# A mixture of 16,384 experts: routing starts inside the last projections, and 192 of 256 tokens are scattered by indirect transfers

## The chip, the core and the metric

The kernel runs on one core of a Trainium2 chip. The core's engines work side by side, each through its own queue of instructions: TensorE (PE) multiplies matrices, VectorE (DVE) and ScalarE (ACT) work elementwise, GpSimd (POOL) issues the indirect DMAs and does some elementwise work, SyncE (SP) issues the other DMAs. They wait for one another through semaphores. The metric is the device time of one execution in microseconds (us); less is better.

## What is computed

One decoder layer on 256 tokens of width 1024, all in float32: a mixer (a gated linear recurrence beside block-sparse attention), cross-attention into 256 memory tokens, and a channel mixer of 128 x 128 single-neuron experts (PEER). The change touches the last alone, of which this is the core:

```python
def peer_ffn(xn, w_q, sub_keys, u, v):            # T = 256 tokens, 8 heads, 128 keys, top 16
    q = (t @ w_q).reshape(T, PEER_HEADS, 2, PEER_HALF)
    s = jnp.einsum('thpd,hpnd->thpn', q, sub_keys)
    s_top, i_top = lax.top_k(s, PEER_TOPK)
    cand_s = s_top[:, :, 0, :, None] + s_top[:, :, 1, None, :]          # 16 x 16 sums
    cand_i = i_top[:, :, 0, :, None] * PEER_KEYS + i_top[:, :, 1, None, :]
    best_s, pos = lax.top_k(cand_s, PEER_TOPK)
    ids = jnp.take_along_axis(cand_i, pos, axis=-1)
    gates = jax.nn.softmax(best_s, axis=-1)
    act = jax.nn.gelu(jnp.einsum('td,ted->te', x_c, u[ids_c]), approximate=False)
    return jnp.einsum('te,ted->td', g_c * act, v[ids_c])
```

A token thus needs 8 heads x 16 ranks = 128 of the 16,384 experts, each with a gate.

## The kernel before

**Dense experts.** The kernel computes all experts for all tokens. A matrix A of 16,384 experts x 256 tokens (act_w, 128 keys of 128 experts) gets gelu(u t), is multiplied by a map of gates that is zero where a token doesn't use an expert, and is then multiplied with v. Every float32 product is made of three matmuls: both operands are split into a high part, which ACT copies in a rounded type, and a low part, which DVE subtracts.

**Projections.** 38 units of 256 columns (L1109), 48 matmuls each. SP loads a unit's weights into one of four buffers, ACT writes the high part (wsp, L395), DVE the low one (L714; GpSimd for two units). Units 30 to 37 make the PEER queries. Then come 32 matmuls of key scores (L1258), which ACT copies out, and the residual as a seed in the accumulators of V.

**Stage U, 128 keys.** Each key takes 24 matmuls of 256 columns (L1273 to L1275). SP loads two keys' weights at a time (raw), ACT writes the high part (hl, L625) and the GELU (L630), DVE the low part (hl, L937). Four buffers hold split keys.

**Routing, woven into U.** DVE does the top-16 work in 64 parts, four per head and tile of 128 tokens: the 16 best rows, the 16 best columns (L941 to L953), the 256 candidate sums and their best (L957 and on), and index and logit (L962 to L978). A table puts 8 parts into 11 keys. ACT takes the exponential, DVE normalizes it (gate_norm, L984 to L986).

- Tile 0: one indirect DMA on GpSimd (L370) adds 128 tokens' gates of one head and rank into a map in HBM (wmap, 8 MB, zeroed by four stores of SP). That is 128 DMAs, and before each head GpSimd waits for the head before (s_scattered), since two heads may meet in one cell.
- Tile 1: after key 92 PE transposes the gates (L1310); from key 95 on, each key carries one of 32 groups of four tokens: DVE and ACT write one-hot rows and columns (oh_i L994, oh_j L642 and L646, each fourth on DVE), PE multiplies them (L1299), DVE applies the result to A (place, L1008). Columns of keys that come later get their GELU through a buffer (late, L634 and L1016).

**Stage V.** For every two keys SP loads a block of the map (wblk, L306 and L314) as soon as all scatters have landed, GpSimd weighs A with it (L376), ACT and DVE write A's high and low parts (whl, L677 and L1050), and PE does 12 matmuls of 512 columns per key (L1324). Then follow the final norm and the store.

The order on each engine is the order in which its block of code issues. The functions that the diff touches:

Of the kernel before, what the change touches and what calls it, by code (L numbers as in the profile page):

```python
# [58 lines left out]
NGRP = P // GRP  # L59
NZERO = 4  # L60
WBK = 2
NWB = KEYS // WBK
BATCHES = ((0, 1), (1, 3), (3, PH))
# [4 lines left out]
def build(nc, x, mem, par, wa, wx, w, keys_t, u_t, v, g_final, wmap, out):  # L68
    ctx = ExitStack()
    with ctx:  # L70
# [30 lines left out]
        zeros = at("zeros", m + 2 * K, [512])  # L101
        krow = at("krow", m, [3, P])
# [3 lines left out]
        kt3 = at("kt3", m, [3, P])  # L106
        late = at("late", m + 1536, [2, P])
        wblk = at("wblk", m + 2560, [2, WBK, P])
# [9 lines left out]
        sumf = at("sumf", m + 2 * K + 1280, [TOPK])  # L118
        m += 4 * K + 512
        gate = at("gate", m, [PH, TOPK]); m += 512  # L120
        widx = at("widx", m, [PH, TOPK], U32); m += 512
# [59 lines left out]
        s_sca = sem("s_scattered")  # L181
        s_kt, s_kte = sem("s_key_cols_mm"), sem("s_key_cols")
        s_ojd = sem("s_onehot_j_dve")
# [42 lines left out]
        def part_key(n):  # L226

            return -(-11 * (n + 1) // 8) - 1

        def pass_key(n):  # L230

            return part_key(4 * n + 3)
# [6 lines left out]
        wm = wmap.rearrange("(i j t) o -> i j (t o)", i=KEYS, t=P)  # L239
# [9 lines left out]
        def dve_j(g):  # L249

            return (g + 1) // 4

        def placed(j):

            return GRP * max(0, min(NGRP, j + 1 - ROUTE0))

# [4 lines left out]
        def _(sp):  # L261
# [17 lines left out]
            sp.wait_ge(s_const, 9)  # L279
# [4 lines left out]
            for u in range(WRAW, NU):  # L284
                unit(u)
                if u % 2 == 0 and u // 2 - U_CK // 2 in range(NZERO):
                    z = (u - U_CK) // 2
                    n = KEYS * P // 512 // NZERO
                    sp.dma_start(wz[:, z * n:z * n + n], zeros[:].unsqueeze(1).broadcast_to([P, n, 512])).then_inc(s_zero, 16)
                if u == U_PQ + 4:  # L290
                    sp.dma_start(keys[:], keys_t).then_inc(s_keys, 16)
# [12 lines left out]
            sp.wait_ge(s_sca, 16 * TOPK * PH)  # L304
# [18 lines left out]
        def _(pool):  # L323
# [15 lines left out]
            nc.gpsimd.iota(tcol[:, 0:1], pattern=[[1, 1]], base=0, channel_multiplier=1,  # L339
                           allow_small_or_imprecise_dtypes=True).then_inc(s_const, 1)  # L340
# [23 lines left out]
            for b, (h0, h1) in enumerate(BATCHES):  # L364
                pool.wait_ge(s_gr, b + 1)
                for h in range(h0, h1):
                    if h:
                        pool.wait_ge(s_sca, 16 * TOPK * h)
                    for k in range(TOPK):
                        nc.gpsimd.indirect_dma_start(  # L370
                            out=wmap, out_offset=bass.IndirectOffsetOnAxis(ap=widx[:, h, k:k + 1], axis=0),
                            in_=gate[:, h, k:k + 1], in_offset=None, compute_op=ALU.add).then_inc(s_sca, 16)
# [17 lines left out]
        def _(act):  # L390
# [77 lines left out]
            act.wait_ge(s_const, 9)  # L468
# [142 lines left out]
            for u in range(U_PQ, NU):  # L611
                unit(u)
            sr = srow[:].rearrange("p (t h) a k -> p t (h a k)", t=TT)
            for n in range(8):
                act.wait_ge(s_ks, n + 1)
                nc.scalar.activation(sr[:, n // 4, 512 * (n % 4):512 * (n % 4) + 512], bank[n % 4][:], ACT.Copy).then_inc(s_ke, 1)


# [18 lines left out]
            def onehots_j(g):  # L637
                t0, slot = group_token(g), g % 2
# [6 lines left out]
                act.wait_ge(s_ojq, g + 1 - dve_j(g))  # L645
                nc.scalar.activation(oh_j[:, slot], oh_j[:, slot], ACT.Relu, scale=-1.0, bias=ones[:, 0:1]).then_inc(s_oja, 1)  # L646

            act.wait_ge(s_pv, HEADS + CHEADS)
            for k in range(4):
                split_high(k, 16 if k % 2 == 0 else None, (s_seed, 1) if k == 2 else None, s_uh)  # L650
            act.wait_ge(s_zero, 16 * NZERO)

            exps = 0
            for j in range(KEYS):
# [6 lines left out]
                if exps < len(BATCHES) and j == pass_key(BATCHES[exps][1] - 1) + 2:  # L661
                    h0, h1 = BATCHES[exps]
                    act.wait_ge(s_rt, h1)
                    nc.scalar.activation(gate[:, h0:h1], gate[:, h0:h1], ACT.Exp).then_inc(s_ge, 1)
                    exps += 1
                if j == pass_key(TT * PH - 1) + 1:
                    act.wait_ge(s_rt, TT * PH)
                    nc.scalar.activation(krow[:, 2], krow[:, 2], ACT.Exp).then_inc(s_ge, 1)
                if j == WEAVE:
                    act.wait_ge(s_kt, 1)  # L670
                    nc.scalar.activation(kt3[:].rearrange("p a t -> p (a t)"), bank[2][:, 0:3 * P], ACT.Copy).then_inc(s_kte, 1)
                    act.wait_ge(s_kte, 1)
                if 0 <= j - (ROUTE0 - 2) < NGRP and (j - (ROUTE0 - 2)) % 4 < 3:
                    onehots_j(j - (ROUTE0 - 2))

            def a_high(j, slot):
                nc.scalar.activation(whl[:, slot, 0], act_w[:, ds(j, 1)].rearrange("p o t -> p (o t)"), ACT.Copy).then_inc(s_Wh, 1)  # L677

            split_high(3, None, (s_um, KEYS), s_vh, second=True)
            act.wait_ge(s_gw, NGRP)  # L680
            for k in range(4):
                if k % WBK == 0:
                    act.wait_ge(s_A, k // WBK + 1)
                a_high(k, k)
# [17 lines left out]
        def _(dve):  # L702
# [228 lines left out]
            for u in range(U_PQ, NU):  # L931
                unit(u)


# [12 lines left out]
            def route_part(n, part):  # L947

                t, h = n // PH, n % PH
                if part < 2:  # L950
                    best16(srow[:, PH * t + h, part], rwork[:], part)
                    if t == 0:
                        link(V.tensor_scalar(topf[:, part], topi[:, part], float(P * (1 if part else KEYS)), None, ALU.mult))  # L953
                    else:
                        link(V.tensor_copy(topf[:, part], topi[:, part]))
# [5 lines left out]
                else:  # L961
# [7 lines left out]
                    if t == 0:  # L969
                        link(V.tensor_reduce(sumf[:], eq[:].rearrange("p a k b -> p k a b"), XY, ALU.add))  # L970
                        link(V.tensor_scalar(widx[:, h], sumf[:], tcol[:, 0:1], None, ALU.add))
                        logits = gate[:, h]
                    else:
                        ks = slice(TOPK * h, TOPK * h + TOPK)
                        link(V.tensor_reduce(krow[:, 0:2, ks], eq[:], X, ALU.add))
                        logits = krow[:, 2, ks]
                    V.tensor_scalar(logits, topv[:, 2], topv[:, 2, 0:1], None, ALU.subtract).then_inc(s_rt, 1)

            def gate_norm(n, ex):

                dve.wait_ge(s_ge, n + 1)
                k = ex.shape[1]
                gs = stat[:, GS:GS + k]
                link(V.tensor_reduce(gs, ex, X, ALU.add))  # L984
                link(V.reciprocal(gs, gs))
                V.tensor_tensor(ex, ex, gs.unsqueeze(2).broadcast_to([P, k, TOPK]), ALU.mult).then_inc(s_gr, 1)  # L986

            def onehots_i(g):
                t0, slot = group_token(g), g % 2
# [7 lines left out]
                if g % 4 == 3:  # L997
                    V.tensor_tensor(oh_j[:, slot], iota[:].unsqueeze(1).broadcast_to([P, GRP, P]),
                                    kt3[:, 1, t0:t0 + GRP].unsqueeze(2).broadcast_to([P, GRP, P]), ALU.is_equal).then_inc(s_ojd, 1)

            def place(g):

                dve.wait_ge(s_gm, g + 1)
                j0, c = ROUTE0 + g, P + group_token(g)
# [13 lines left out]
            for k in range(4):  # L1018
                split_low(k, s_ul, (s_uh, k + 1))
            dve.wait_ge(s_ke, 8)  # L1020
            dve.wait_ge(s_zero, 16 * NZERO)


            parts = normed = 0
            for j in range(KEYS):
                if j < KEYS - 4:
                    split_low(j % 4, s_ul, (s_uh, j + 5))
                elif j < KEYS - 1:
                    split_low(j % 4, s_vl, (s_vh, j + 5 - KEYS), second=True)
                if normed < len(BATCHES) and j == pass_key(BATCHES[normed][1] - 1) + 4:  # L1030
                    h0, h1 = BATCHES[normed]
                    gate_norm(normed, gate[:, h0:h1])
                    normed += 1
                if j == pass_key(TT * PH - 1) + 3:
                    gate_norm(normed, krow[:, 2].rearrange("p (h k) -> p h k", k=TOPK))
# [3 lines left out]
                if 0 <= j - ROUTE0 < NGRP:  # L1039
                    place(j - ROUTE0)  # L1040
# [4 lines left out]
                if 0 <= j - (ROUTE0 - 2) < NGRP:  # L1045
                    onehots_i(j - (ROUTE0 - 2))
# [5 lines left out]

            split_low(3, s_vl, (s_vh, 4), second=True)
            for k in range(4):
                a_low(k, k)
# [318 lines left out]
```

## Time and profile before

| | |
|---|---|
| median of three runs | 1067.56 us (1065.86 to 1069.15) |
| the profiled execution's own time | 1069.02 us |
| its span in the trace | 1067.0 us |
| mean granted TensorE clock | 0.987 |
| busy: PE / DVE / ACT / POOL | 97 / 68 / 54 / 27% |
| projections up to the key scores | 0 to 293 us |
| stage U | 304 to 707 us |
| stage V and the end | 710 to 1067 us |

A row of a timeline gives start and duration in us, engine, line, operation and tiles, and in brackets the idle time of that engine ahead of it and what ended it. A count (x8) behind a row joins like instructions.

### The profile page before, as it was taken

How to read it: one execution, taken by the hardware profiler on the slowest of the kernel's cores; microseconds unless marked ns; L12 is line 12 of the kernel's file. 1: busy time of each engine (PE TensorE's matmuls, PEld its weight loads, DVE VectorE, ACT ScalarE, POOL GpSimd, SP SyncE). 2: the span in 40 equal slices, each digit the busy share in tenths (PEclk: the TensorE clock that was granted, in tenths of full speed). 3: DMA queues.
4: the chain of work that ended last, by engine and by line, in shares of the span. 5: the costliest groups of instructions: out<-in, count | busy, mean ns of one | idle time of the engine just before them, and what ended most of it. 6: DMA issues, size and time to landing. Idle time of an engine off the chain costs nothing.

```text
span 1067.0 us, 19322 instructions
## 1 busy us (share of the span) xinstructions
PE 1036.6 (97%) x7019; PEld 960.4 (90%) x7019; DVE 729.4 (68%) x1439; ACT 574.8 (54%) x988; POOL 289.0 (27%) x215
## 2 busy tenths in 40 slices
PE   6999999999999999999999999989999999999997
PEld 6988899899999999999999999978888888888886
DVE  5765566544349999999997888865555555555554
ACT  6784555544365544534446778745445554455543
POOL 1000001010002788577778650011111111111110
PEclk9998999998999999999999999989999999999999
DMA  9598444426234766666666553446666566666662
GB/s 318 166 316 287 148 142 148 145 80 194 83 119 158 197 160 196 178 176 185 181 186 182 137 157 129 149 158 214 213 213 216 211 219 217 221 221 221 217 214 95
DMA packets 92480, 196.56 MB, mean 184 GB/s; under 512 B 23569, under 2 KB 70673, under 8 KB 75921
## 3 DMA queue, kind: packets, MB, share of 16 engines
q1 hardware_dynamic: 74000, 195.87, 52.9%
q0 software_dynamic: 18432, 0.07, 3.9%
q8 instruction: 28, 0.46, 0.2%
q14 instruction: 20, 0.16, 0.0%
HBM read 186.42 MB, written 9.50 MB: 184 GB/s over the span
## 4 chain that ended last, share of the span: by engine, by line
PE 70%; DVE 20%; DMA 4%; ACT 4%; issue 1%; SPq 0%; DVEq 0%; ACTq 0%
PE acc L1324 33%; PE acc L1109 19%; DVE hl L937 6%; PE bank L1273 4%; PE bank L1274 4%; PE bank L1275 4%; DMA raw<-u_t 4%; PE bank L1299 3%; DVE hl3u L937 2%; DVE topv L943 1%; DVE eq L965 1%; DVE eq L968 1%; ACT hl L625 1%; DVE topi L944 1%; DVE topi L945 1%
## 5 line engine op out<-in xcount | busy, mean ns | idle before, releaser
L937 DVE TENSOR_TENSOR hl<-raw,hl 128x1024 fp32r<-128x1024 f32 x192 | 234.4, 1226 | 152.6 <-ACT hl L625 150.8
L625 ACT ACTIVATE hl<-raw 128x1024 fp32r<-128x1024 f32 x192 | 203.3, 1059 | 232.6 <-PE acc L1324 130.3
L1324 PE MATMUL acc<-hl,whl 128*128 128x512 f32 x1152 | 269.2, 392 | 3.2 <-DVE whl L1050 3.2
L370 POOL DMA_INDIRECT wmap<-gate,widx x128 | 219.7, 1716 | 173.7 <-DVE gate L986 109.8
L1324 PEld LDWEIGHTS acc<-hl,whl 128*128 128x128 f32 x1152 | 218.0, 189 | 48.9 <-DVE hl3v L937 3.3
L1273 PE MATMUL bank<-xt,hl 128*128 128x256 f32 x768 | 220.8, 287 | 0.6 <-DVE hl L937 0.5
L1274 PE MATMUL bank<-xt,hl 128*128 128x256 f32 x768 | 217.8, 284 | 0.0
L1275 PE MATMUL bank<-xt,hl 128*128 128x256 f32 x768 | 217.8, 284 | 0.0
L376 POOL TENSOR_TENSOR act_w<-act_w,wblk 128x256 f32 (+1 forms) x64 | 51.4, 803 | 364.2 <-DMA wblk<-wmap 296.9
L1273 PEld LDWEIGHTS bank<-xt,hl 128*128 128x128 f32 x768 | 147.9, 193 | 1.5 <-issue 1.2
L1274 PEld LDWEIGHTS bank<-xt,hl 128*128 128x128 f32 x768 | 148.0, 193 | 0.2 <-issue 0.2
L1275 PEld LDWEIGHTS bank<-xt,hl 128*128 128x128 f32 x768 | 147.8, 192 | 0.0
L714 DVE TENSOR_TENSOR wsp<-wraw,wsp 128x2048 fp32r<-128x2048 f32 x35 | 80.2, 2290 | 77.1 <-ACT wsp L395 76.9
L1109 PE MATMUL acc<-xt,wsp 128*128 128x256 f32 x960 | 120.7, 289 | 2.5 <-DVE xt L735 2.5
L1109 PEld LDWEIGHTS acc<-xt,wsp 128*128 128x128 f32 x960 | 119.4, 197 | 3.6 <-issue 3.5
L395 ACT ACTIVATE wsp<-wraw 128x2048 fp32r<-128x2048 f32 x35 | 66.9, 1913 | 85.1 <-PE acc L1109 85.1
L1324 PE MATMUL acc<-hl3v,whl 128*128 128x512 f32 x384 | 92.4, 389 | 0.0
L1324 PEld LDWEIGHTS acc<-hl3v,whl 128*128 128x128 f32 x384 | 72.1, 188 | 15.0
L630 ACT ACTIVATE act_w<-bank 128x256 f32<-128x256 f32 (+11 forms) x128 | 46.4, 363 | 66.4 <-PE bank L1275 66.1
L1273 PE MATMUL bank<-xt,hl3u 128*128 128x256 f32 x256 | 73.2, 286 | 0.2 <-DVE hl3u L937 0.2
L1275 PE MATMUL bank<-xt,hl3u 128*128 128x256 f32 x256 | 72.4, 283 | 0.0
L1274 PE MATMUL bank<-xt,hl3u 128*128 128x256 f32 x256 | 72.4, 283 | 0.0
(219 smaller groups left out, 1325.4 us busy)
## 6 DMA issues: line engine op xcount, KB each, us to landing
raw<-u_t SPq DMA_DIRECT2D x64, 1024.0 KB, 4.9
raw<-v SPq DMA_DIRECT2D x64, 1024.0 KB, 4.9
wraw<-w_in SPq DMA_DIRECT2D x9, 1024.0 KB, 8.3
wmap<-zeros SPq DMA_DIRECT2D x4, 2048.0 KB, 11.6
wraw<-w_pq SPq DMA_DIRECT2D x8, 1024.0 KB, 5.3
wblk<-wmap SPq DMA_DIRECT2D x64, 128.0 KB, 4.6
wraw<-w_ck SPq DMA_DIRECT2D x4, 1024.0 KB, 7.7
wraw<-w_cv SPq DMA_DIRECT2D x4, 1024.0 KB, 6.5
```

What stands on the lines that cost most here:

```text
L370: nc.gpsimd.indirect_dma_start(out=wmap, out_offset=bass.IndirectOffsetOnAxis(ap=widx[:, h, k:k + 1], axis=0), in_=gate[:, h, k:k + 1], in ...
L376: nc.gpsimd.tensor_tensor(aw, aw, wblk[:, q], ALU.mult).then_inc(s_A, 1)
L395: nc.scalar.activation(wsp[:, u % 2, 0], wraw[:, u % WRAW], ACT.Copy).then_inc(s_wh, 1)
L625: nc.scalar.activation(eslot(k, 0, second), raw[:, k // 2, k % 2], ACT.Copy).then_inc(ready, 1)
L630: last = nc.scalar.activation(aw[:, 0:T - n], ubank(j)[:, 0:T - n], ACT.Gelu)
L714: V.tensor_tensor(wsp[:, u % 2, 1], wraw[:, u % WRAW], wsp[:, u % 2, 0].bitcast(F32), ALU.subtract).then_inc(s_wl, 1)
L937: V.tensor_tensor(eslot(k, 1, second), raw[:, k // 2, k % 2], eslot(k, 0, second).bitcast(F32), ALU.subtract).then_inc(ready, 1)
L1109: last = pe.matmul(dst, a, b, start=(c == c0 and n == 0), stop=(c == c1 - 1 and n == 2))
L1273: pe.matmul(dst, uh[:, c], xt[:, c, 0], start=(c == 0), stop=False)
L1274: pe.matmul(dst, uh[:, c], xt[:, c, 1], start=False, stop=False)
L1275: last = pe.matmul(dst, ul[:, c], xt[:, c, 0], start=False, stop=(c == DC - 1))
L1324: last = pe.matmul(acc[:, 2 * t + n], a, b[:, 512 * n:512 * n + 512], start=False, stop=last_key and k == 2, skip_group_check=True)
```

## The change

- **Key scores and routing start earlier.** The scores of a head (now both tiles at once) are made right behind the projection unit that follows it, so the keys are loaded in the projections already. 14 of the 64 route parts (3.5 heads of tile 0) and two gate steps stand on DVE between the weight splits of units 30 to 37 and the first operand splits of U. The other parts keep their pace of 8 in 11 keys and so end at key 68 instead of 87.
- **192 tokens are scattered.** The map is 192 tokens wide (WT; 12 MB, zeroed by six stores). Tile 0 goes as two sets of 64 tokens x 2 ranks, so a DMA still carries 128 cells and a head takes two times 8; tokens 128 to 191 go as two sets of 32 tokens x 4 ranks, two times 4 for a head. That makes 192 DMAs. Each set has a semaphore, and a head waits for the same set of the head before. The gate step (gates) also computes the address and copies gates and addresses into the sets' layout: 8 small copies for tile 0, 16 for tile 1.
- **One-hots for the last 64 tokens alone**, 16 groups, one at every second key from 95 to 125; all their columns on ACT.
- **Stage V's blocks and the weighing** are 192 tokens wide instead of 128, and SP waits for all four sets.
- **The high and low parts of A for the first four keys** are written behind key 126, ahead of the last key's GELU and split, once their weighing and the last one-hot group are done.

```diff
-NZERO = 4
+HT = P // 2
+NGRP = HT // GRP
+WT = P + HT
+NZERO = 6
-BATCHES = ((0, 1), (1, 3), (3, PH))
+SETS = ((0, 0, 64, 8), (0, 64, 64, 8), (1, 0, 32, 4), (1, 32, 32, 4))
+BATCHES = ((0, 0, 1), (0, 1, 3), (0, 3, 5), (0, 5, PH), (1, 0, PH))
+PARTS0 = 14
...
-            return -(-11 * (n + 1) // 8) - 1
+            return -(-11 * (n - PARTS0 + 1) // 8) - 1
...
-            sp.wait_ge(s_sca, 16 * TOPK * PH)
+            for k, (_, _, _, nr) in enumerate(SETS):
+                sp.wait_ge(s_sca[k], 16 * nr * PH)
...
-            for b, (h0, h1) in enumerate(BATCHES):
+            for b, (t, h0, h1) in enumerate(BATCHES):
                 pool.wait_ge(s_gr, b + 1)
                 for h in range(h0, h1):
-                    if h:
-                        pool.wait_ge(s_sca, 16 * TOPK * h)
-                    for k in range(TOPK):
...
+                    for k in (2 * t, 2 * t + 1):
+                        nr = SETS[k][3]
+                        if h:
+                            pool.wait_ge(s_sca[k], 16 * nr * h)
+                        for r in range(nr):
...
-                aw = act_w[:, ds(b * WBK, WBK), 0:P]
+                aw = act_w[:, ds(b * WBK, WBK), 0:WT]
...
+            def gates(b):
+
+                t, h0, h1 = BATCHES[b]
+                n, ks = h1 - h0, slice(TOPK * h0, TOPK * h1)
+                link(V.scalar_tensor_tensor(dest[:, ks], krow[:, t, 0, ks], float(KEYS), krow[:, t, 1, ks], ALU.mult, ALU.add))
+                link(V.tensor_scalar(dest[:, ks], dest[:, ks], float(WT), tcol[:, t:t + 1], ALU.mult, ALU.add))
+                dve.wait_ge(s_ge, b + 1)
...
+                link(V.tensor_tensor(ex, ex, gs.unsqueeze(2).broadcast_to([P, n, TOPK]), ALU.mult))
+                for k in (2 * t, 2 * t + 1):
+                    _, t0, nt, nr = SETS[k]
+                    for r in range(TOPK // nr):
...
+                        V.tensor_copy(set_ranks(gate, k)[p, h0:h1], ex[src, :, rs])
+                        last = V.tensor_copy(set_ranks(widx, k)[p, h0:h1], to[src, :, rs])
+                last.then_inc(s_gr, 1)
...
+            for u in range(U_PQ, NU - 2):
+                unit(u)
+                if u == U_PQ + 4:
+                    gates(0)
+                    route_parts(6, 7)
+                elif u > U_PQ:
+                    p0 = 2 * (u - U_PQ - 1) if u < U_PQ + 5 else 7
+                    route_parts(p0, p0 + 2)
+            split_low(0, s_ul, (s_uh, 1))
+            route_parts(9, 12)
+            split_low(1, s_ul, (s_uh, 2))
+            route_parts(12, PARTS0)
+            gates(1)
+            for k in (2, 3):
...
+                if j == KEYS - 2:
+                    act.wait_ge(s_gw, NGRP)
+                    for k in range(4):
+                        if k % WBK == 0:
+                            act.wait_ge(s_A, k // WBK + 1)
+                        a_high(k, k)
...
+            for u in range(U_PQ + 1, NU):
+                unit(u, xt)
+                if u < NU - 1:
+                    key_scores(u - U_PQ - 1)
```

Three places show what stands in a row on an engine. First GpSimd, where the scatter begins; s_gates counts gate steps, s_scattered the landed DMAs (with a number: those of a set). Before:

```order
L370 DMA wmap<-gate,widx 2097152x1 [waits s_gates,s_zeroed]
L370 DMA wmap<-gate,widx 2097152x1 x15
L370 DMA wmap<-gate,widx 2097152x1 [waits s_scattered,s_gates]
L370 DMA wmap<-gate,widx 2097152x1 x15
L370 DMA wmap<-gate,widx 2097152x1 [waits s_scattered]
```

And now:

```order
L380 DMA wmap<-gate,widx 3145728x1 [waits s_gates,s_zeroed]
L380 DMA wmap<-gate,widx 3145728x1 x15
L380 DMA wmap<-gate,widx 3145728x1 [waits s_scattered0,s_gates]
L380 DMA wmap<-gate,widx 3145728x1 x7
L380 DMA wmap<-gate,widx 3145728x1 [waits s_scattered1]
L380 DMA wmap<-gate,widx 3145728x1 x7
```

The wait for the head before now looks back over eight DMAs of the other set.

Second VectorE, in the last projection units. Before, weight splits (wsp) run straight into the operand splits of U (hl), and the first top-16 (topv) comes behind six of them:

```order
L714 TENSOR_TENSOR wsp<-wraw,wsp 128x2048 [waits s_w_high] x7
L937 TENSOR_TENSOR hl<-raw,hl 128x1024 [waits s_u_high] x2
L937 TENSOR_TENSOR hl_54<-raw,hl_54 128x1024 [waits s_u_high]
L937 TENSOR_TENSOR hl3u<-raw,hl3u 128x1024 [waits s_u_high]
L937 TENSOR_TENSOR hl<-raw,hl 128x1024 [waits s_u_high,s_zeroed,s_key_rows]
L937 TENSOR_TENSOR hl<-raw,hl 128x1024 [waits s_u_high]
L941 MAX topv<-srow 128x8
```

Now, between two weight splits, this is the first gate step, which follows six route parts (two of its four pairs of copies are shown):

```order
L735 TENSOR_TENSOR wsp<-wraw,wsp 128x2048 [waits s_w_high,s_dve_chain]
L993 SCALAR_TENSOR_TENSOR dest<-krow 128x16
L994 TENSOR_SCALAR dest<-dest,tcol 128x16 [waits s_dve_chain]
L999 TENSOR_REDUCE stat<-krow 128x1 [waits s_gate_exp,s_dve_chain]
L1000 RECIPROCAL stat<-stat 128x1 [waits s_dve_chain]
L1001 TENSOR_TENSOR krow<-krow,stat 128x16 [waits s_dve_chain]
L1006 COPY gate<-krow 64x8 [waits s_dve_chain]
L1007 CAST widx<-dest 64x8
L1006 COPY gate<-krow 64x8
L1007 CAST widx<-dest 64x8
```

The first weight split of a later unit now waits behind such steps, and so do U's operand splits.

Third ScalarE, at the end of U. Before:

```order
L625 ACTIVATE hl_54<-raw 128x1024 [waits s_u_mm,s_raw1]
L630 ACTIVATE act_w<-bank 128x128 [waits s_u_mm]
L634 ACTIVATE late<-bank 128x128 [waits s_late_gelu_used]
L625 ACTIVATE hl3v<-raw 128x1024 [waits s_u_mm]
L677 ACTIVATE whl<-act_w 128x256 [waits s_weighed,s_route_placed]
L677 ACTIVATE whl<-act_w 128x256
L677 ACTIVATE whl<-act_w 128x256 [waits s_weighed]
L677 ACTIVATE whl<-act_w 128x256
```

And now:

```order
L639 ACTIVATE hl_54<-raw 128x1024 [waits s_u_mm,s_raw1]
L679 ACTIVATE whl<-act_w 128x256 [waits s_weighed,s_route_placed]
L679 ACTIVATE whl<-act_w 128x256
L679 ACTIVATE whl<-act_w 128x256 [waits s_weighed]
L679 ACTIVATE whl<-act_w 128x256
L644 ACTIVATE act_w<-bank 128x192 [waits s_u_mm]
L648 ACTIVATE late<-bank 128x64 [waits s_late_gelu_used]
L639 ACTIVATE hl3v<-raw 128x1024 [waits s_u_mm]
```

The four copies of A (whl), with their waits for the weighing and for the last one-hot group, now stand ahead of the last GELU and the last high part.

## Rows read from the trace of the kernel before

**Rows 1.** The page: DMA engines' busy tenths in 40 slices; longest chain by line.

```profile
DMA  9598444426234766666666553446666566666662
...
PE acc L1324 33%; PE acc L1109 19%; DVE hl L937 6%; PE bank L1273 4%; PE bank L1274 4%; PE bank L1275 4%; DMA raw<-u_t 4%; PE bank L1299 3%; DVE hl3u L937 2%; DVE topv L943 1%; DVE eq L965 1%; DVE eq L968 1%; ACT hl L625 1%; DVE topi L944 1%; DVE topi L945 1%
```

**Rows 2.** Timeline of ScalarE at the start of U (start us, us, engine, line).

```profile
312.92 0.39 ACT L630 ACTIVATE act_w<-bank 128x256 f32<-128x256 f32 x1 [0.86 <-PE bank L1275]
...
315.80 0.38 ACT L630 ACTIVATE act_w<-bank 128x256 f32<-128x256 f32 x1 [1.55 <-PE bank L1275]
```

**Rows 3.** Timeline of TensorE at the joints and at two one-hot groups.

```profile
293.44 7.38 PE L1258 MATMUL bank<-keys,qpt 128*128 128x128 f32 x64 [0.84 <-ACT qpt L408]
...
575.83 0.85 PE L1310 MATMUL bank<-ident,krow 128*128 128x128 f32 x3 [1.92 <-DVE krow L986]
...
695.61 1.06 PE L1299 MATMUL bank<-oh_j,oh_i 128*128 128x128 f32 x8
...
699.38 1.06 PE L1299 MATMUL bank<-oh_j,oh_i 128*128 128x128 f32 x8
...
710.23 6.07 PE L1324 MATMUL acc<-hl,whl 128*128 128x512 f32 x14 [3.17 <-DVE whl L1050]
```

**Rows 4.** Windows: us, busy PE PEld DVE ACT POOL (instructions), PEclk, DMA, GB/s.

```profile
575.80:579.50 3.70, 3.67 (x18) 3.67 (x19) 1.11 (x1) 0.75 (x1) 3.09 (x3) 0.54 1.05 352
...
716.00:1060.00 344.00, 344.00 (x1520) 284.82 (x1518) 195.40 (x252) 172.14 (x253) 49.88 (x62) 1.00 0.59 208
```

**Rows 5.** Timeline of GpSimd: the first transfer, two around 580, the last.

```profile
338.53 1.69 POOL L370 DMA_INDIRECT wmap<-gate,widx  x1 [99.12 <-DVE gate L986]
...
580.47 2.01 POOL L370 DMA_INDIRECT wmap<-gate,widx  x1 [0.30 <-issue]
582.79 2.09 POOL L370 DMA_INDIRECT wmap<-gate,widx  x1 [0.30 <-issue]
...
631.19 1.54 POOL L370 DMA_INDIRECT wmap<-gate,widx  x1 [0.30 <-issue]
```

**Rows 6.** Timeline of VectorE: last weight split, first routing and gate step.

```profile
283.13 2.29 DVE L714 TENSOR_TENSOR wsp<-wraw,wsp 128x2048 fp32r<-128x2048 f32 x1 [3.47 <-ACT wsp L395]
...
313.25 0.29 DVE L941 MAX8 topv<-srow 128x8 f32<-128x128 f32 x1
...
315.15 1.23 DVE L937 TENSOR_TENSOR hl<-raw,hl 128x1024 fp32r<-128x1024 f32 x1
...
321.18 0.42 DVE L957 TENSOR_TENSOR cand<-topv 128x256 f32<-128x256 f32 x1
...
324.01 1.22 DVE L937 TENSOR_TENSOR hl<-raw,hl 128x1024 fp32r<-128x1024 f32 x1
...
325.15 0.17 DVE L962 TENSOR_SCALAR posu<-topi 128x16 uint32<-128x16 uint32 x1
...
328.24 1.22 DVE L937 TENSOR_TENSOR hl<-raw,hl 128x1024 fp32r<-128x1024 f32 x1
...
337.44 0.18 DVE L986 TENSOR_TENSOR gate<-gate,stat 128x16 f32<-128x16 f32 x1
```

**Rows 7.** Waits of GpSimd at the transfers: us in all, times, longest.

```profile
POOL wmap L370 <- issue: 43.4, 120, 3.6
...
POOL wmap L370 <- DMA wmap<-gate,widx: 20.4, 6, 4.2
```

**Rows 8.** Groups by line on GpSimd: busy us, mean ns, idle before.

```profile
L370 POOL DMA_INDIRECT wmap<-gate,widx x128 | 219.7, 1716 | 173.7 <-DVE gate L986 109.8 <-issue 43.4 <-DMA wmap<-gate,widx 20.4
...
L376 POOL TENSOR_TENSOR act_w<-act_w,wblk 128x256 f32 (+1 forms) x64 | 51.4, 803 | 364.2 <-DMA wblk<-wmap 296.9 <-ACT late L634 67.3
```

**Rows 9.** Timeline of VectorE beside the two transfers of rows 5.

```profile
579.85 1.23 DVE L937 TENSOR_TENSOR hl<-raw,hl 128x1024 fp32r<-128x1024 f32 x1 [2.94 <-ACT hl L625]
...
582.24 1.23 DVE L937 TENSOR_TENSOR hl<-raw,hl 128x1024 fp32r<-128x1024 f32 x1 [1.17 <-ACT hl L625]
```

**Rows 10.** DMAs of line L314 (the blocks of the map): issue to landing.

```profile
DMA to landing us min/median/max: 4.3/4.6/8.6
```

More of the change, by code:

```diff
@@ L105, in build @@
         m += 8 * K
-        kt3 = at("kt3", m, [3, P])
-        late = at("late", m + 1536, [2, P])
-        wblk = at("wblk", m + 2560, [2, WBK, P])
+        kt3 = at("kt3", m, [3, HT])
+        late = at("late", m + 768, [2, HT])
+        wblk = at("wblk", m + 1280, [2, WBK, WT])
         cand = at("cand", m, [256])
@@ L117, in build @@
         topf = at("topf", m + 2 * K + 1152, [2, TOPK])
-        sumf = at("sumf", m + 2 * K + 1280, [TOPK])
+        dest = at("dest", m + 3 * K + 512, [PH * TOPK])
         m += 4 * K + 512
-        gate = at("gate", m, [PH, TOPK]); m += 512
-        widx = at("widx", m, [PH, TOPK], U32); m += 512
+        gate = at("gate", m, [WT]); m += 768
+        widx = at("widx", m, [WT], U32); m += 768
         tcol = at("tcol", m, [8]); m += 32
@@ L180, in build @@
         s_zero = sem("s_zeroed")
-        s_sca = sem("s_scattered")
+        s_sca = [sem(f"s_scattered{i}") for i in range(len(SETS))]
         s_kt, s_kte = sem("s_key_cols_mm"), sem("s_key_cols")
-        s_ojd = sem("s_onehot_j_dve")
         s_oi, s_ojq, s_oja, s_gm, s_gw, s_fx = (sem(n) for n in (
@@ L610, in _, with key_rows, gate_exp @@
             after_norm(U_PQ - 1, 3, "ln_ffn")
[L611 to L616, printed above, removed]
+            sr = srow[:].rearrange("p (t h) a k -> p t h (a k)", t=TT)
+            def key_rows(h):
+                act.wait_ge(s_ks, h + 1)
+                nc.scalar.activation(sr[:, :, h], bank[h % 4][:].rearrange("p (t n) -> p t n", t=TT), ACT.Copy).then_inc(s_ke, 1)
+            def gate_exp(b):
+                t, h0, h1 = BATCHES[b]
+                act.wait_ge(s_rt, PH * t + h1)
+                ex = krow[:, t, 2, TOPK * h0:TOPK * h1]
+                nc.scalar.activation(ex, ex, ACT.Exp).then_inc(s_ge, 1)
             def split_high(k, landed, free, ready, second=False):
@@ L930, in _ @@
             unit(U_PQ - 1)
-            for u in range(U_PQ, NU):
-                unit(u)
             def split_low(k, ready, have, second=False):
@@ L950, in route_part @@
                 if part < 2:
+                    if part == 0 and t == 0:
+                        dve.wait_ge(s_ke, h + 1)
                     best16(srow[:, PH * t + h, part], rwork[:], part)
[L952 to L955, printed above, removed]
+                    link(V.tensor_copy(topf[:, part], topi[:, part]))
                 elif part == 2:
@@ L1029, in _ @@
                     split_low(j % 4, s_vl, (s_vh, j + 5 - KEYS), second=True)
[L1030 to L1035, printed above, removed]
+                if batches < len(BATCHES) and j == batch_key(batches) + 4:
+                    gates(batches)
+                    batches += 1
                 if parts < 4 * TT * PH and j == part_key(parts):
@@ L1245, in _, with key_scores, seed @@
             unit(U_PQ, xt, (s_tl, 3 * DC))
-            for u in range(U_PQ + 1, NU):
-                unit(u, xt)
             pe.wait_ge(s_keys, 16)
-            wevac(pe, NU - 1)
-            for t in range(TT):
-                for b in range(4):
-                    n = 4 * t + b
-                    if n >= 4:
-                        pe.wait_ge(s_ke, n - 3)
-                    for k in range(4):
-                        hp = 4 * b + k
-                        last = pe.matmul(bank[b][:, P * k:P * k + P], qpt[:, hp, P * t:P * t + P], keys[:, hp], start=True, stop=True)
-                    last.then_inc(s_ks, 1)
-            for t in range(TT):
+            def key_scores(h):
+                wevac(pe, U_PQ + h)
+                if h >= 4:
+                    pe.wait_ge(s_ke, h - 3)
+                for t in range(TT):
+                    for a in range(2):
+                        c = T * t + KEYS * a
+                        last = pe.matmul(bank[h % 4][:, c:c + KEYS], qpt[:, 2 * h + a, P * t:P * t + P], keys[:, 2 * h + a],
+                                         start=True, stop=True)
+                last.then_inc(s_ks, 1)
+            def seed(t):
                 for n in range(2):
```

165 lines of the change are left out of this document (81 added, 84 removed).

## The prediction

> **What bounds the kernel now.** I read the page's chain by line first, then TensorE's timeline at the joints between stages, then the queue that the change loads most, GpSimd's. The chain is TensorE nearly throughout: the value stage (acc L1324) 33%, the projections (L1109) 19%, and where VectorE's split (hl L937) stands in the chain, TensorE is busy beside it [rows 1]. So TensorE has a floor of instructions and a few joints where it waits. One U key takes 2.88 us: two GELUs lie that far apart [rows 2]. A key that carries a one-hot group takes 3.77 [rows 3], so a group costs 0.89. Two joints are dear. After key 92 TensorE waits 1.92 us for the last gates, and the granted clock then stands at 0.54 for 3.7 us, near the lower level of 1.2 GHz: 18 matmuls take 3.67 us where 18 x 0.12 = 2.2 is the pace: 1.5 lost, 3.4 together [rows 3, 4]. From U to V it waits 3.17 us, and the first 14 value matmuls take 6.07, where 344 us for 1520 is the pace, 3.2 for 14: 2.9 lost, 6.0 together [rows 3, 4]. GpSimd ends its 128 indirect transfers at 631.19 + 1.54 = 632.7, some 75 us before V asks for them [rows 5]: today it is far off the path.
>
> **What the change takes off TensorE.** 16 of 32 one-hot groups: 16 x 0.89 = 14.2. The wait behind key 92: the last gates now come at DVE's key 72, 20 keys before the transposes, so the 3.4 goes. The 0.84 wait ahead of the key scores [rows 3]: the scores go into the projection units, their 7.38 us and the seeds' time stay, 0.8 goes. The joint U to V: high and low parts of A for keys 0 to 3 move ahead of GELU 127, so 3.2 of wait goes if the weighed activations are there, and the 2.9 of slow clock with it. Together 14.2 + 3.4 + 0.8 + 6.0 = 24.4 us.
>
> **What it puts on VectorE.** In the last units VectorE idles 3.47 of every 5.76 us (3.47 + 2.29) [rows 6]. That is the cover for 14 route parts and two gate steps, and it isn't enough. A top-16 part is 315.15 - 313.25 = 1.90, the candidates' 324.01 - 321.18 = 2.83, the last part 3.09, without its widx step 2.8 [rows 6]. From 283.13 - 4 x 5.76 = 260.1 on, five weight splits (2.29 each, 11.5), 14 parts (8 x 1.90 + 3 x 2.83 + 3 x 2.8 = 32.1), two gate steps and three operand splits (3.5) stand in one row. A gate step is not in the trace as it will be: the old one is three operations of about 0.2 [rows 6]; the new one has 13 small ones, so 0.5 to 3; I take 1.8, 13 at 0.14. The third split is then done at 260.1 + 11.5 + 32.1 + 3.6 + 3.5 + 0.6 of small waits = 311.4. Key 2, whose GELU is at 312.92 in before, starts a key's 2.88 and a little sooner, at 309.8 [rows 2]; now 0.8 earlier, 309.0: a stall of 2.4, with a clock loss like the one above, 1.5. Later gate steps fall into VectorE's fullest stretch, but the parts end at key 68, not 87; this cancels, within 2. So TensorE alone would begin V at 710.2 - 14.2 - 3.4 - 3.2 - 0.8 + 3.9 = 692.5.
>
> **What it puts on GpSimd** decides, I think. 192 transfers stand in for 128. The first follows gate step 0: 260.1 + four weight splits 9.2 + six parts 13.2 + 0.6 + 1.8 = 284.9, and 0.9 on, as 338.53 stands behind the end of the old step at 337.62 [rows 5, 6]: 285.8. From there the queue never runs dry, and the waits for the head before, 20.4 us in six [rows 7], go, since eight (four) transfers of the other set lie between. The mean transfer is 1.72 [rows 8] plus 0.30 of issue, but the shortest are 1.54, 1.84 with the issue [rows 5], and the rest is a mechanism: a transfer that starts while a two-input split runs on VectorE waits for its end. The split at 579.85 ends at 581.08; the transfer of 580.47 ends 1.40 after that, and the next starts at 582.79, 1.71 after it [rows 5, 9]. Three stretches follow.
> (a) To 518 VectorE is full of parts (50 parts 119, 69 splits 84, two steps 3.6, from 312). I take 2.04, the 2.02 of before and a little for the gates: 232 / 2.04 = 114 transfers.
> (b) To 579 (key 93) VectorE has one split a key. A split ends, the next begins 2.88 - 1.23 = 1.65 later, the transfer asks at 1.71, just inside it, and is held to its end again: one transfer a key. Until VectorE has caught up I take 2.3 over 26 us, then 2.88 over 35: 23 transfers.
> (c) To 691, a group every second key: 2.88 + 3.77 = 6.65 hold three transfers (held, free, held), 2.22 each: 50.
> That is 187; five more with VectorE idle at 1.84 end at 700. Longer gaps come on top: issue gaps sum to 43.4 in 120, 7.4 over 0.30 each, the longest 3.6 [rows 7]; 192 transfers make it 11, and what falls into a hold is free: I take 6, bounds 0 and 14. The last ends at 706. Behind it: 3.4 to its landing (20.4 / 6), 4.6 for wblk [rows 10], a weighing of 0.80 x 1.5 = 1.2 [rows 8], and the high and low parts, 0.9 (the old joint's 3.17 less a copy and a split): 10.1. V begins at 716, not 710.2: **5.8 us later**. TensorE has then been idle for 25 us, so the slow first matmuls stay.
>
> The Trainium skill's page "SBUF — State Buffer", in "SBUF: two separate sides", says that VectorE and GpSimd share one port pair as an exclusive lock for a whole instruction, and warns of VectorE's copies in a 2-port mode that keep GpSimd from writing a DMA's descriptors. The trace agrees on the lock, with 1.40 us of a transfer left after the split's end. The warning names the copies alone; by those alone each transfer would take 1.84, the last end at 639, and V begin at 692.5. The rows show two-input splits that hold the queue, so the rows decide.
>
> **What I cost at nothing.** Two more zero stores lie beside the w_out loads, where the DMA engines are 40% busy (slices 5 to 8) [rows 1]; one late weight load there would cost some us. The 50% larger wblk and weighing lie under V, where TensorE is busy 344 of 344 us [rows 4]; a wblk buffer has two key pairs, 10.9 us, for 4.6 + 1.2 and the issue. Exp steps move with their gates, five against four.
>
> **The rivals.** First, on the other side, GpSimd in time: if the holds of (b) and (c) don't lock and 2.02 lasts, 285.8 + 192 x 2.02 + 6 = 680, V is ready at 690 and TensorE's 692.5 counts: 17.7 earlier and no slow clock, 2.9: 1067.6 - 20.6 = 1047. For it: the mean held at 2.02 over a varied trace. Against it: that stretch has routing on VectorE throughout. It decides once the last transfer ends before 682. Second, GpSimd late but by less: no long gaps and 2.0 in (c): end at 690 to 699, V at 700 to 709, time 1057 to 1066. Third, worse: long gaps twice as many, or 2.88 from 518 on: end at 715, V at 725, 1082. Fourth, the early one-hot values don't do what they say: the ACT wait for the weighed pairs now stands ahead of GELU 127 and the last split; behind a late GpSimd all of these queue. That is in the forecast, since V needs the pairs first anyway.
>
> **How the numbers follow.** The profiled execution took 1069.02 with a span of 1067.0, 1.5 above the median, 1067.56. The sum moves the span to 1072.8, the execution to 1074.8, the median to 1073.4; I say 1073. Chances: forecast 0.56, GpSimd in time 0.13, late by less 0.22, worse 0.09. The range reaches to the second and third: 1056 to 1082, leaving out the first and a tail. 0.3%, 3.2 us, is about what a measurement of this kernel can tell from no change. Faster by more than that: 0.13 and half of "late by less", 0.25; within: the rest of it and the forecast's lower part, 0.23; slower: 0.52.
>
> **What the profile after would show.** The first transfer near 286; 114 done by 518; starts 2.88 apart between 545 and 579 and three per 6.65 from there; the last end near 706; then wblk, weighing, and the first value matmul at 716 behind an idle of 25 us. A stall at U key 2 of about 2.4; none behind key 92; 16 groups of 0.89. I am wrong if transfers keep a pace of 2.0 after 518, or if TensorE waits for VectorE for more than 5 us in U.

## The result, and the profile after

The changed kernel takes 1058.97 us (1056.94 to 1061.39) against 1067.68 for the kernel before in the same runs, a ratio of 0.9927 with a 95% interval of 0.991 to 0.9944. It is 0.7% faster where I forecast 0.5% slower. The profiled execution has a span of 1059.6 us against 1067.0.

The chain of the changed kernel, from the page, shows first what happened: GpSimd's transfers (L380) now hold a third of the span, where TensorE and VectorE held it before [rows 1].

```profile
PE 53%; POOL 33%; issue 6%; DVE 4%; ACT 2%; DMA 1%; SPq 0%; DVEq 0%; ACTq 0%; POOLq 0%
PE acc L1362 33%; POOL wmap L380 33%; PE acc L1142 16%; DVE wsp L735 1%; ACT wsp L405 1%; DMA wraw<-w_in 1%; DVE xs L751 1%; PE bank L1246 1%; PE bank L1224 0%; PE bank L1171 0%; DMA wmap<-gate,widx 0%; PE bank L1154 0%; PE bank L1153 0%; PE bank L1112 0%; DMA wblk<-wmap 0%
```

GpSimd's groups and waits of the changed kernel answer [rows 7, 8]. The queue waits for nothing but its own issue between the first transfer and the last; the waits for the head before are gone.

```profile
L380 POOL DMA_INDIRECT wmap<-gate,widx x192 | 350.5, 1825 | 105.9 <-issue 59.9 <-DVE widx L1007 46.1
```

```profile
POOL wmap L380 <- issue: 59.9, 191, 2.0
```

Its timeline, at the start, in the middle of U and at the end, answers [rows 5], and VectorE's beside the middle answers [rows 9]. The first transfer starts at 285.69. In the middle a transfer starts 0.06 behind a split's start, takes 2.58 instead of 1.54, and the next comes 2.88 later, again 0.06 behind a split's start. The last one ends at 696.05.

```profile
285.69 1.69 POOL L380 DMA_INDIRECT wmap<-gate,widx  x1 [46.05 <-DVE widx L1007]
...
563.70 2.58 POOL L380 DMA_INDIRECT wmap<-gate,widx  x1 [0.30 <-issue]
566.58 2.58 POOL L380 DMA_INDIRECT wmap<-gate,widx  x1 [0.30 <-issue]
569.46 2.58 POOL L380 DMA_INDIRECT wmap<-gate,widx  x1 [0.30 <-issue]
...
694.43 1.62 POOL L380 DMA_INDIRECT wmap<-gate,widx  x1 [0.30 <-issue]
700.18 1.94 POOL L386 TENSOR_TENSOR act_w<-act_w,wblk 128x384 f32<-128x384 f32 x2 [4.13 <-DMA wblk<-wmap]
```

```profile
563.64 1.22 DVE L954 TENSOR_TENSOR hl<-raw,hl 128x1024 fp32r<-128x1024 f32 x1 [1.66 <-ACT hl L639]
566.52 1.23 DVE L954 TENSOR_TENSOR hl3u<-raw,hl3u 128x1024 fp32r<-128x1024 f32 x1 [1.66 <-ACT hl3u L639]
```

TensorE's timeline at U's key 2, at key 33 and at the joint to V answers [rows 3]. It waits 3.63 and 1.90 for VectorE's splits and 7.72 for the first value operands, which wait for the map.

```profile
312.33 0.38 PE L1314 MATMUL bank<-xt,hl 128*128 128x256 f32 x1 [3.63 <-DVE hl L954]
...
405.38 0.38 PE L1314 MATMUL bank<-xt,hl 128*128 128x256 f32 x1 [1.90 <-DVE hl L954]
...
702.55 9.74 PE L1362 MATMUL acc<-hl,whl 128*128 128x512 f32 x29 [7.72 <-DVE whl L1061]
```

So the start of V moved from 710.23 to 702.55, 7.7 us, nearly the whole change of the span (7.4). It is made of 1.3 from an earlier first key (less than executions of one kernel differ by), 10.9 from a shorter U (403.4 to 392.4), and 4.6 given back in the wait before V (3.17 to 7.72).

### The profile page after: what moved, and what is told of

Read it like the earlier page. It is cut to its first block, busy times and chain, and to the rows that moved or that the text cites. A ratio compares the mean times of both kernels' runs of the same rounds, so it can differ in the third digit from the quotient of the medians.

```text
span 1059.6 us, 19013 instructions
## 1 busy us (share of the span) xinstructions
PE 1020.5 (96%) x6891; PEld 944.7 (89%) x6891; DVE 703.6 (66%) x1388; ACT 559.7 (53%) x948; POOL 434.1 (41%) x280
## 4 chain that ended last, share of the span: by engine, by line
PE 53%; POOL 33%; issue 6%; DVE 4%; ACT 2%; DMA 1%; SPq 0%; DVEq 0%; ACTq 0%; POOLq 0%
PE acc L1362 33%; POOL wmap L380 33%; PE acc L1142 16%; DVE wsp L735 1%; ACT wsp L405 1%; DMA wraw<-w_in 1%; DVE xs L751 1%; PE bank L1246 1%; PE bank L1224 0%; PE bank L1171 0%; DMA wmap<-gate,widx 0%; PE bank L1154 0%; PE bank L1153 0%; PE bank L1112 0%; DMA wblk<-wmap 0%
## 5 line engine op out<-in xcount | busy, mean ns | idle before, releaser
L380 POOL DMA_INDIRECT wmap<-gate,widx x192 | 350.5, 1825 | 105.9 <-issue 59.9
L386 POOL TENSOR_TENSOR act_w<-act_w,wblk 128x384 f32 (+1 forms) x64 | 65.6, 1026 | 279.5 <-DMA wblk<-wmap 279.5
```

Of the source, the lines that this page charges most:

```text
L380: nc.gpsimd.indirect_dma_start(out=wmap, out_offset=bass.IndirectOffsetOnAxis(ap=set_ranks(widx, k)[:, h, r:r + 1], axis=0), in_=set_ranks ...
```

## Experiments

My theory was that the last indirect transfer sets the start of V, and that VectorE's two-input splits set the pace of the transfers. The rivals were that TensorE's own time, or something else at the end of U, sets it, and that the pace of one transfer a key has another cause. The projections end up to 3 us earlier or later from one execution to the next, so the traces are compared from U's first matmul on. The last column runs from the start of the first value matmul to the start of the fifteenth. All numbers are us:

| kernel | time | U's first to V's first matmul | last transfer's end, from U's first | wait before V | first 14 value matmuls |
|---|---|---|---|---|---|
| before | 1066.6 to 1067.7 | 406.5 | 329.0 | 3.17 | 5.9 |
| changed | 1058.97 | 400.2 | 393.7 | 7.72 | 6.1 |
| changed, 16 transfers fewer | 1051.8 | 392.4 | 358.1 | 0.43 | 3.3 |
| changed, early A operands undone | 1058.67 | 398.0 | 390.7 | 4.76 | 5.7 |
| changed, halved splits | 1050.06 | 393.3 | 365.0 | 0.50 | 3.3 |
| changed, second gate step later | 1056.59 | 398.8 | 392.5 | 7.55 | 5.3 |
| halved, 12 early parts | 1046.3 | 388.9 | 362.5 | 0.5 | 3.3 |
| halved, 12 early parts, slower pace | 1042.31 | 384.2 | 365.2 | 0.50 | 3.3 |
| the same, early A operands undone | 1046.39 | 386.9 | 365.2 | 3.17 | 6.0 |
| before, early A operands alone | 1062.37 | 404.3 | 329.2 | 0.65 | 3.3 |

### Sixteen transfers fewer

```diff
-                for h in range(h0, h1):
+                for h in range(h0, h1 - 2 * t):
```

(SyncE's count of landed transfers is lowered to match.)

> The changed kernel without the last 16 of its 192 indirect transfers (heads 6 and 7 of tokens 128 to 191 get no gate, so that part of the output is left out). Theory: the value stage begins when the last transfer has landed. Then the queue ends near 661 instead of 696, TensorE goes from U to V without a wait worth naming (under 1 us, at 695 instead of 702.55), the slow first value matmuls go as well, and the time is 1048 to 1052. Rival: the 7.7 us wait has another cause (the block load, the weighing, the order on ScalarE); then V stays at 702.5 and the time at 1059.

The time is 1051.8 us, a ratio of 0.9857 (0.9833 to 0.9882) to the kernel before. The last transfer ends at 659.09. TensorE's timeline at the joint:

```profile
693.36 8.43 PE L1362 MATMUL acc<-hl,whl 128*128 128x512 f32 x36 [0.43 <-DVE whl L1061]
```

The wait is 0.43 and the slow first matmuls are gone: the granted clock is 1.00 from 693.4 to 697.0. Nothing else at the end of U was changed, so the wait of 7.72 was for the transfers and what follows the last of them; the rival falls.

### Early operands of A undone

```diff
             split_high(3, None, (s_um, KEYS), s_vh, second=True)
+            act.wait_ge(s_gw, NGRP)
+            for k in range(4):
+                if k % WBK == 0:
+                    act.wait_ge(s_A, k // WBK + 1)
+                a_high(k, k)
```

(The same loop at key 126 goes, and VectorE's with it.)

> The changed kernel with the high and low parts of A for keys 0 to 3 put back behind the last key's GELU and split. Theory (the indirect transfers set the start of V): nothing is gained or lost, V at 702.5 within 0.5, time within 2 us of 1059. Rival (the early split is worth the 3 to 6 us that I gave to this joint): V some 2 to 3 us later, time 1062 to 1065.

1058.67 us against 1058.97 is no difference: this part of the change does nothing while the map is late. V's own start is at 698.90, outside the half microsecond that I allowed: U began 1.5 earlier and the last transfer ended 2.9 earlier as counted from there, in this one execution. V follows it by 7.3 us, against 6.5 with the early operands, so they save 0.8 behind the last transfer, which the times don't show.

### Halved splits

```diff
+                n = D // pieces
+                for i in range(pieces - 1):
+                    c = slice(n * i, n * i + n)
+                    V.tensor_tensor(eslot(k, 1, second)[:, c], raw[:, k // 2, k % 2, c], eslot(k, 0, second)[:, c].bitcast(F32),
+                                    ALU.subtract)
...
-                    split_low(j % 4, s_ul, (s_uh, j + 5))
+                    split_low(j % 4, s_ul, (s_uh, j + 5), pieces=PIECES if j >= 70 else 1)
```

> The changed kernel with VectorE's operand split of the keys from 74 on issued as two instructions of 512 columns instead of one of 1024. Theory (a transfer that starts while a two-input VectorE instruction runs is held to its end, which locks the queue to one transfer per 2.88 us key): the hold is at most 0.6, starts in the stretch 555 to 584 lie about 1.9 apart instead of 2.88, the last transfer ends near 680 and V begins at 695; time 1048 to 1052. Rival (one transfer per key comes from something else of a key's period, such as the 1 MB weight loads): starts stay 2.88 apart, V stays at 702 and the time at 1059.

1050.06 us, a ratio of 0.9847 (0.9828 to 0.9867). The last transfer ends 28.7 us earlier from U's first matmul on, V waits 0.50, with all 192 transfers there. The end, 665.8, is earlier than the 680 that I expected, since beside the groups the pace fell as well, from 2.2 to 1.9. GpSimd's and VectorE's timelines between 556 and 563 show the mechanism:

```profile
556.78 1.97 POOL L381 DMA_INDIRECT wmap<-gate,widx  x1 [0.31 <-issue]
559.06 1.54 POOL L381 DMA_INDIRECT wmap<-gate,widx  x1 [0.30 <-issue]
560.91 1.54 POOL L381 DMA_INDIRECT wmap<-gate,widx  x1 [0.30 <-issue]
562.75 1.77 POOL L381 DMA_INDIRECT wmap<-gate,widx  x1 [0.30 <-issue]
```

```profile
556.65 0.69 DVE L958 TENSOR_TENSOR hl<-raw,hl 128x512 fp32r<-128x512 f32 x1 [1.59 <-ACT hl L640]
557.26 0.68 DVE L961 TENSOR_TENSOR hl<-raw,hl 128x512 fp32r<-128x512 f32 x1
...
562.41 0.69 DVE L958 TENSOR_TENSOR hl<-raw,hl 128x512 fp32r<-128x512 f32 x1 [1.59 <-ACT hl L640]
```

The transfer of 556.78 starts inside the first half, which ends at 557.34, and ends 1.41 after it, at 558.75, although the second half runs until 557.94: it slips in at the end of one instruction, and is not held by the next. Three transfers now go with two keys: 15 start between 555 and 584, 1.94 apart, where the changed kernel has 11, 2.88 apart. The weight loads and the key's 2.88 us are as before, so the rival falls. The halves cost VectorE 0.15 us a key (2 x 0.69 against 1.23), where it is idle anyway.

Halving shortens the instruction and leaves its two inputs, so by itself it doesn't show that the inputs matter. The rows of the changed kernel bear on that. All 70 transfers that start at least 0.05 us after a split's start and 0.14 before its end end 1.40 to 1.43 after that split. In the routing there are two instructions of the same length, a compare with two inputs (L981) and a reduction with one (L986). Three transfers start inside the compare, with 0.44 to 0.61 of it left, and take 1.86 to 2.02; five start inside the reduction, with 0.40 to 0.57 left, and all take 1.54. One of each, VectorE's row first:

```profile
470.17 0.69 DVE L981 TENSOR_TENSOR eq<-posf,iota 128x512 f32<-128x512 f32 x1
470.25 2.02 POOL L380 DMA_INDIRECT wmap<-gate,widx  x1 [0.30 <-issue]
...
486.90 0.69 DVE L986 TENSOR_REDUCE krow<-eq 128x32 f32<-128x512 f32 x1
487.05 1.54 POOL L380 DMA_INDIRECT wmap<-gate,widx  x1 [0.30 <-issue]
```

### The second gate step later

```diff
-            split_low(1, s_ul, (s_uh, 2))
-            route_parts(12, PARTS0)
-            gates(1)
-            for k in (2, 3):
+            for k in (1, 2, 3):
                 split_low(k, s_ul, (s_uh, k + 1))
+            route_parts(12, PARTS0)
...
+                if j == 0:
+                    gates(1)
```

> The changed kernel with the first four operand splits of U ahead of route parts 12 and 13, and the second gate step behind key 0's split. Theory: the stall of 3.6 us at U's key 2 shrinks below 1.5 and U ends 3 to 5 us earlier, but the indirect transfers end where they did (696 within 2), so V begins at 702 within 2 and the time stays 1059 within 2. Rival (TensorE's own time sets the start of V): the time falls with U's end, to 1054 to 1056.

The stall at key 2 goes, but others take its place, at keys 7, 17, 18 and 55, and U is 1.2 us shorter, not 3 to 5. Part of this expectation failed: the stalls that came elsewhere, in the stretch that VectorE's routing fills up to key 68, took back most of the gain. The groups of TensorE's waits for splits in this run sum to 5.3, where the changed kernel has the 5.5 of its two:

```profile
PE acc L1362 <- DVE whl L1059: 7.5, 1, 7.5
PE bank L1314 <- DVE hl L954: 4.5, 4, 1.8
...
PE bank L1314 <- DVE hl3u L954: 0.8, 2, 0.4
```

By the clock of the trace V is at 698.19 and the last transfer's end at 691.87, outside the 2 us around 702 and 696 that I allowed; U began 3.0 earlier, and from there the transfers end within 1.2 of the changed kernel. V still waits 7.55 for the map and begins 6.3 behind the last transfer, so it is still GpSimd that sets its start. 1056.59 us lies beside the rival's 1054 to 1056, 2.4 under the changed kernel, but the intervals of the two (0.9888 to 0.9942, and 0.991 to 0.9944) overlap, so no gain is shown; it is the trace that speaks against the rival, not the time.

### Twelve early parts, and a slower pace

With the splits halved the last transfer ends 28 us ahead of V. The path behind it takes 6 to 7, so some 21 us are to spare, and these two give VectorE's work more room.

```diff
-PARTS0 = 14
+PARTS0 = 12
```

> The kernel with the halved operand splits (from key 74 on), and with 12 instead of 14 route parts ahead of U, at the same pace of 8 in 11 keys. With GpSimd in time, TensorE's own time counts, and there the stall at U's key 2 (3.8, and 1.6 of slow clock behind it) is the largest loss. Theory: VectorE has two parts (3.8 us) less ahead of key 2, so that stall goes; but 8 parts and 11 splits (32.7 us) don't fit into 11 keys (31.7), so some of it comes back later as short stalls, as in the run with the late gate step. U takes 390 to 391 us instead of 392.8, time 1047 to 1050. Rival: the stalls do not come back; U 387.5, time 1045.

1046.3 us, and U 4.4 us shorter than with the halves alone, between the theory and its rival: stalls come back at keys 21, 26, 36 and 37, 3.2 us together (the one of 1.12 is put down to ScalarE's GELU, the others to VectorE's splits), less than what goes at keys 2, 33 and 77, 6.0 of waits and 1.6 of slow clock (the expectations name the last two by the key ahead, 32 and 76). Then:

```diff
-            return -(-11 * (n - PARTS0 + 1) // 8) - 1
+            return -(-12 * (n - PARTS0 + 1) // 8) - 1
```

> As the run with 12 parts, and the route parts at 8 in 12 keys (halved splits from key 82 on). Theory: 8 parts and 12 splits (33.9 us) fit into 12 keys (34.6), so the stalls at keys 2, 32 and 76 go; U takes 384 to 386 us; tile 1's gates come near 540, when tile 0's transfers are just done, and the last transfer ends near 670, still in time; V at 685 to 687; time 1041 to 1045. Rival: the later gates let GpSimd run dry or end too late, V behind a wait again, time 1050 or more.

1042.31 us, a ratio of 0.9775 (0.975 to 0.98), and 1040.76 on another chip:

> The kernel with halved splits, 12 early parts and 8 parts in 12 keys once more, beside the run with the early operand split undone on the same chip: 1042 within 1.5 us.

(ratio 0.9758, 0.9734 to 0.9782). This is the version that beats both the kernel before and the changed one. TensorE's waits show that none is left for a split in U, and 0.5 before V; the chain, from the page, is TensorE's nearly alone.

```profile
PE acc L1369 <- DVE whl L1068: 0.5, 1, 0.5
```

```profile
PE 93%; DVE 3%; ACT 2%; DMA 1%; issue 0%; SPq 0%; DVEq 0%; ACTq 0%
```

### Early operands of A, where the map is in time

First this part of the change alone, in the kernel before:

```diff
+                if j == KEYS - 2:
+                    act.wait_ge(s_gw, NGRP)
+                    for k in range(4):
+                        if k % WBK == 0:
+                            act.wait_ge(s_A, k // WBK + 1)
+                        a_high(k, k)
```

(VectorE's four splits move in the same way.)

> The kernel before, with one part of the change alone: high and low parts of A for keys 0 to 3 written behind key 126, ahead of the last GELU and split. By my term of 6.0 us for this joint (3.2 of wait, 2.9 of slow clock) the time would be 1061. By the rows of before the last one-hot group is applied at 706.7, so ScalarE's four copies and VectorE's four splits end near 708.5, with V's first matmul at 707.6 to 708.3 instead of 710.23; whether a wait of 1 us still brings the slow clock is open: 1062 if not, 1065 if so.

1062.37 us, ratio 0.9962 (0.9947 to 0.9977): 4.2 us. From U's first matmul on V comes 2.2 earlier, and the first value matmuls run at full clock. Then undone in the best version:

> The kernel with halved splits, 12 early parts and 8 parts in 12 keys, with the early operand split undone: the same edit that changed nothing while GpSimd was late. Theory: with the map in time, the order on ScalarE and VectorE at the end of U counts, as in the kernel before: TensorE waits about 3 us between U and V (0.50 with the early split) and the first 14 value matmuls take about 6 us instead of 3.3; time 1046 to 1048 against 1042.3. Rival: the joint has other slack by now; time within 1.5 us of 1042.3.

1046.39 us against 1040.76 on the same chip: 5.6 us. TensorE's timelines at the joint, the kernel before with it:

```profile
705.27 8.41 PE L1326 MATMUL acc<-hl,whl 128*128 128x512 f32 x36 [0.65 <-DVE whl L1027]
```

and the best version without it:

```profile
689.32 11.16 PE L1367 MATMUL acc<-hl,whl 128*128 128x512 f32 x36 [3.17 <-DVE whl L1067]
```

The same edit is worth nothing in the changed kernel and 4 to 6 us on either side of it. It pays as soon as the map is in time, somewhat less than the 6.0 of my sum.

## Why the prediction was wrong

The mechanism was right, and it still decided: GpSimd's last transfer sets the start of V. Three terms of the sum for that transfer were mis-sized, all the same way, and that turned the sign.

| step of GpSimd's sum | forecast | measured |
|---|---|---|
| first transfer starts | 285.8 | 285.69 |
| transfers started by 518 | 114 | 113 |
| 518 to 579 | 23 | 27 |
| 579 to 691 | 50 | 50 |
| long gaps, over 0.30 each | 6 | 1.7 |
| last transfer ends | 706 | 696.05 |
| to SP's first block load | 3.4 | 1.6 |
| block load, to the weighing | 4.6 | 2.5 |
| weighing and operands, to V | 2.1 | 2.4 |
| V begins | 716 | 702.55 |

**The first transfer and stretches (a) and (c)** hold to within a transfer: the queue's start was a sum of 260.1 and VectorE's parts, the pace of three per two keys with a group came from the rule of the held transfer alone, and both were measured as forecast. (Inside (c) the rows show one long hold in three transfers, 2.57, 1.61 and 1.54, where I had two; the sum of the three is the same.)

**Stretch (b)** is the first step that failed: four transfers more than I gave it, three more over all, so that 5.5 us less remained behind U. I let the lock, one transfer a key, set in at 544 and took 2.3 for the stretch before it. It set in at 555. Until then VectorE's rows show no regular split: after the last routing part at 519 come idle stretches, tile 1's gate step with its 16 copies (527.76 to 531.8), then two splits in one go. Transfers start 2.03 apart there. From 555.06 on they stand 2.88 apart, as I had it.

**The long gaps** were the second: 6 taken, 1.7 measured, 4.3 us. The kernel before had three of them; here is one, of 1.98, at 518.48, and no run of the changed kernel's kind had more than 2.6 us over 0.30 in all. My scaling by the number of transfers (7.4 to 11) had no mechanism under it, and the bound 0 that I had set beside it was the better end. What makes these gaps was not tried and stays open.

**The path behind the last transfer** was the third: 6.5 instead of 10.1. I took both times from where other work lay beside them: the 3.4 from GpSimd's waits for a head (20.4 in six) [rows 7], the 4.6 from block loads that share the queue with V's weight loads [rows 10]. Here no such load runs beside the first two: SyncE issues the next one at 699.74. The other runs bear out the second: the first two block loads land after 2.3 to 2.5 where they are late (early operands undone, second gate step later) and after 4.8 to 4.9 where they come on time, right behind two of V's weight loads (16 transfers fewer, and the halved splits). Why the first is 1.6 and not 3.4 was not tried. SyncE's rows and the line of its first block loads in the changed kernel show 696.05 to 697.67 for the first and a landing after 2.4 for the second:

```profile
697.67 0.80 SPq L313 DMA_DIRECT2D wblk<-wmap  x2
```

```profile
DMA to landing us min/median/max: 2.4/2.4/2.5
```

5.5 + 4.3 + 3.6 = 13.4, next to the 13.45 of 716 less 702.55. The one long gap lies ahead of 518.48, so its 1.7 is in the count of 113 already, and the first two terms are each good to about one transfer; what is firm is their sum, 706 less 696.05.

**TensorE's part** was closer: without GpSimd I had V ready at 692.5, and U ends at 694.8. The 16 groups gave 0.88 each, the joint behind key 92 is gone as forecast (its key takes 3.13), and at key 2 the wait was 3.63 instead of 2.4, with 1.6 of slow clock behind it. Not in the sum were the stalls at key 33 (1.90) and key 77 (0.54), behind later gate steps, which I had set against the earlier end of the parts "within 2". In the changed kernel all of that is hidden behind the 7.7 us of waiting for GpSimd. Both signs of being wrong that I had named showed: a pace near 2.0 after 518, until 555, and 5.5 us of TensorE's waits for VectorE in U, where I had drawn the line at 5.

**The rivals.** The measured time is that of "late by less" (1057 to 1066), which I gave 0.22: fewer gaps were part of its condition, the pace of 2.0 in (c) was not met (2.21 was measured), so its number came out by luck in part. "GpSimd in time" came true only in the runs that made it so: with 16 transfers fewer, or halved splits, V begins as TensorE is ready, and the time is 1050 to 1052, 3 to 5 above the 1047 that I gave that case. By the copies alone, the warning that I had weighed from the Trainium skill's page "SBUF — State Buffer" ("SBUF: two separate sides"), the queue would have ended at 639; it ended at 696, and shortening nothing but two-input subtracts moved it by 28.7 us. The shared lock that the page tells of agrees with that: its rule there also names VectorE's operations with two SBUF inputs, against a GpSimd operation that reads SBUF. Which of GpSimd's accesses to SBUF is held no run here shows.

## What to carry to other kernels

A queue of GpSimd's DMAs beside a regular VectorE instruction with two inputs can fall into step with it, as here: look whether each transfer starts just behind the start of the same instruction, and if so cut that instruction in two before you cut the number of transfers. Take the price of a step from a row in the same company that it will have: a landing that was read under load (4.6) was too dear where the queue was empty (2.4). And an edit that measures as nothing behind a late resource may be worth its whole price once that resource is in time, so undo it only after the bound has moved.

## What the runs showed of the hardware

A transfer that starts inside a two-input split, at least 0.05 us behind its start and 0.14 before its end, ends 1.40 to 1.44 us after that split, in the kernel before, the changed one and the one with halved splits, even when the next half follows at once; so two halves of 0.69 hold the queue less than one of 1.23. Inside a reduction with one input, 0.40 to 0.57 before its end, it takes the same 1.54 as with VectorE idle.

TensorE's granted clock did not fall after each wait. The windows of the changed kernel (busy PE, PEld, DVE, ACT, POOL, then PEclk, DMA share, GB/s) behind the waits of 3.63 (key 2), 1.90 (key 33) and 7.72 (V):

```profile
312.70:316.20 3.50, 3.50 (x19) 3.50 (x18) 3.47 (x5) 0.00 (x0) 2.96 (x2) 0.51 0.53 113
...
405.40:409.40 4.00, 4.00 (x33) 4.00 (x34) 3.83 (x9) 0.00 (x0) 3.39 (x3) 1.00 0.70 244
703.00:708.00 5.00, 5.00 (x13) 3.85 (x13) 1.77 (x4) 1.16 (x3) 0.33 (x1) 0.50 0.87 311
```

0.51 and 0.50 stand at the lower level, 1.2 GHz, 1.00 at the upper, 2.4 GHz. So 1.90 us of wait in the middle of a run of matmuls cost only itself, while 3.17 before V, in the kernel before and in the best version without early operands, brought the slow first matmuls with it (6 us for 14 instead of 3.3). The length of the wait alone doesn't tell the two apart: in the kernel before 1.92 us behind key 92 stood ahead of a granted clock of 0.54 [rows 3, 4]. What does was not tried.
